# Other byte residues for the matmuls' normalised inputs and activations

## The reference

```python
# first block, per layer l (DEPTH = 2, D_MODEL = 1024, SEQ = 256)
h = rms_norm(x, norm_mix_g[l])
p = h @ w_in[l]                        # 1024 x 2832: convolution, attention, gated linear attention
y = concatenate([y_a, y_b, y_c])       # y_a, y_b, y_c: the three mixers on columns of p
x = x + y @ w_out[l]
h = rms_norm(x, norm_ffn_g[l])
u = causal_depthwise_conv(h @ ffn_w_up[l], ...)            # 1024 x 5632, three taps
x = x + (silu(u[..., :2816]) * u[..., 2816:]) @ ffn_w_down[l]
...
# second block, per layer l, for the image x and the context h_ctx
x = swiglu_half_step(x, norm_g[l, 0], mod_x, 0, w_ffn_up[l, 0], w_ffn_down[l, 0])
h_ctx = swiglu_half_step(h_ctx, norm_g[l, 0], mod_c, 0, w_ffn_up[l, 0], w_ffn_down[l, 0])
px, pc = hx @ w_in[l], hc @ w_in[l]    # hx, hc: modulated norms; the same weights for both
...                                    # neighbourhood and windowed attention over image and context
x = x + mod_x[..., 5, :] * (attention @ w_out[l])
x = swiglu_half_step(x, norm_g[l, 2], mod_x, 6, w_ffn_up[l, 1], w_ffn_down[l, 1])
# the same for h_ctx, except in the last layer
```

## Time and profile before

| | us |
|---|---|
| device time, median of 3 runs (2548.97 to 2557.46) | 2553.96 |
| span of the profiled execution, first to last instruction | 2549.3 |
| TensorE, matmuls busy | 2391.4 (94%) |
| TensorE, weight loads busy | 2322.8 (91%) |
| VectorE busy | 1661.0 (65%) |
| ScalarE busy | 997.7 (39%) |
| GpSimd busy | 188.2 (7%) |

### The profile page before, as it was taken

How to read it: one execution, slowest core, us unless ns; L and a number is a source line. 1 busy time by engine, 2 the same in 40 slices (tenths; PEclk the granted TensorE clock), 3 DMA queues, 4 the chain that set the end, 5 groups by cost and what they waited for, 6 DMA issues and landing times. The chain is left out here.

```text
span 2549.3 us, 47682 instructions
## 1 busy us (share of the span) xinstructions
PE 2391.4 (94%) x20452; PEld 2322.8 (91%) x20452; DVE 1661.0 (65%) x2777; ACT 997.7 (39%) x1468; POOL 188.2 (7%) x300
## 2 busy tenths in 40 slices
PE   7989998899799999999788999998999998988999
PEld 7889997899799999899558999998999998967999
DVE  6789888788877777744775677776333336376554
ACT  6455664465432222322473222223222223145543
POOL 0000000370000000011000900000000000100000
PEclk9899998999899999999898999999999999999999
DMA  6246652456445555412001455552222222211454
GB/s 256 95 157 226 221 190 92 144 197 237 141 143 191 188 182 187 169 59 79 14 1 67 164 190 189 186 198 91 92 96 96 100 100 96 70 52 67 162 194 157
DMA packets 104306, 352.78 MB, mean 138 GB/s; under 512 B 18976, under 2 KB 19232, under 8 KB 103840
## 3 DMA queue, kind: packets, MB, share of 16 engines
q1 hardware_dynamic: 95904, 348.94, 38.9%
q0 software_dynamic: 8192, 0.80, 0.3%
HBM read 348.63 MB, written 1.05 MB: 137 GB/s over the span
## 5 line engine op out<-in xcount | busy, mean ns | idle before, releaser
L1456 ACT ACTIVATE W_hi<-W_raw 128x1024 fp32r<-128x1024 f32 x510 | 538.7, 1060 | 1119.6 <-PE slot L930 1053.9
L1830 DVE TENSOR_TENSOR W_lo<-W_raw,W_hi 128x1024 fp32r<-128x1024 f32 x510 | 621.5, 1222 | 473.8 <-ACT W_hi L1456 465.1
L928 PE MATMUL slot<-H_hiA,W_lo 128*128 128x256 f32 x2768 | 790.9, 286 | 18.0 <-DVE H_loA L1960 4.6
L929 PE MATMUL slot<-H_loA,W_hi 128*128 128x256 f32 x2768 | 781.5, 282 | 0.0
L930 PE MATMUL slot<-H_hiA,W_hi 128*128 128x256 f32 x2768 | 780.9, 282 | 0.0
L928 PEld LDWEIGHTS slot<-H_hiA,W_lo 128*128 128x128 f32 x2768 | 533.3, 193 | 29.5 <-issue 21.1
L929 PEld LDWEIGHTS slot<-H_loA,W_hi 128*128 128x128 f32 x2768 | 535.8, 194 | 0.1
L930 PEld LDWEIGHTS slot<-H_hiA,W_hi 128*128 128x128 f32 x2768 | 532.7, 192 | 0.0
L1842 DVE SCALAR_TENSOR_TENSOR PROD<-A_raw,SC 128x1024 bf16<-128x1024 f32 x288 | 341.2, 1222 | 170.3 <-DMA A_raw<-adastream 169.8
L928 PE MATMUL slot<-H_hiB,W_lo 128*128 128x256 f32 x1376 | 385.9, 280 | 3.0 <-DVE VB L2347 1.3
L929 PE MATMUL slot<-H_loB,W_hi 128*128 128x256 f32 x1376 | 383.9, 279 | 0.0
(11 more groups left out here) (277 smaller groups left out, 3057.8 us busy)
## 6 DMA issues: line engine op xcount, KB each, us to landing
W_raw<-wstream SPq DMA_DIRECT2D x510, 512.0 KB, 3.3
A_raw<-adastream SPq DMA_DIRECT2D x144, 512.0 KB, 4.3
BT<-par POOLq DMA_DIRECT2D x256, 3.0 KB, 2.6
XA<-xT SPq DMA_DIRECT2D x2, 512.0 KB, 4.5
SC<-cond SPq DMA_DIRECT2D x1, 1024.0 KB, 14.4
XB<-ctxT SPq DMA_DIRECT2D x1, 1024.0 KB, 16.4
CON<-const SPq DMA_DIRECT2D x1, 960.5 KB, 9.6
PAR<-par SPq DMA_DIRECT2D x1, 680.0 KB, 10.8
```

Source lines behind the costliest of these rows:

```text
L928: pe.matmul(out, wl, xh, start=start, stop=False, skip_group_check=True)
L929: pe.matmul(out, wh, xl, start=False, stop=False, skip_group_check=True)
L1456: act.activation(W_hi[:, g % HIGH, :], W_raw[:, g % RAW, :], ACT.Copy).then_inc(S.w_hi, 1)
L1830: dve.tensor_tensor(W_lo[:, g % RAW, :], W_raw[:, g % RAW, :], W_hi[:, g % HIGH, :].bitcast(F32), ALU.subtract).then_inc(S.w_lo, 1)
```

## The change

A's `H` moves from 192 to 160, B's `H` to 224, A's arena to 32 and B's arena to 96 bytes modulo 256. To make room, what lies behind the arenas moves up by 256 bytes and so keeps its residue: the ring for the modulation's weights `A_raw`, its products `PROD`, the condition `SC`, the small tensors, and `X` of both streams. Nothing else differs.

```diff
-        A_raw = at("A_raw", 166 * K + 256, [P, ADA_RING, UNIT])
-        PROD = at("PROD", 174 * K + 256, [P, 2, UNIT], BF16)
-        SC = at("SC", 178 * K + 256, [P, 2, D])
-        small = [186 * K + 256]
+        A_raw = at("A_raw", 166 * K + 512, [P, ADA_RING, UNIT])
+        PROD = at("PROD", 174 * K + 512, [P, 2, UNIT], BF16)
+        SC = at("SC", 178 * K + 512, [P, 2, D])
+        small = [186 * K + 512]
...
-        AA, AB = 72 * K + 192, 124 * K + 192
-        for s, h_at, x_at, arena in ((A, 40 * K + 192, 150 * K + 256, AA), (B, 56 * K + 192, 158 * K + 256, AB)):
+        AA, AB = 72 * K + 288, 124 * K + 352
+        for s, h_at, x_at, arena in ((A, 40 * K + 160, 150 * K + 512, AA), (B, 56 * K + 224, 158 * K + 512, AB)):
```

## The result

The changed kernel takes 2602.10 us, median of 4 runs (2597.61 to 2607.36), beside 2551.47 us for the kernel before in the same runs (2536.46 to 2557.46, 4 runs). The ratio is 1.0205 with a 95% interval of 1.0157 to 1.0253: slower, by about 50 us. The forecast was 2554.0 us, so the time lies above the range of 2520 to 2588 as well.

The account below looks back on a forecast made before the run. The prediction took TensorE's matmul pace as the bound: long steps costing 27.9 us in joint stages plus 13.0 us solo, 40.9 against 36.2 before, add 4.7 to 2549.3, giving 2554.0 us; range 2520 to 2588.

Parts of the forecast that it names:

- the price of the new residues: TensorE's four moving operands: starting at 32 modulo 64 was taken to cost zero of its own.
- one long step each way: Bound on a new residue's price: -4.3 to +4.3 ns a matmul, the gap between steps of about 113.3 and 117.7 ns.
- The forecast is wrong if a third step appears: Sign of failure: any matmul-to-matmul step besides the short one (113.3 ns) and the long one (about 117.7 ns).
- The bound now: Whole kernel: the pace of TensorE's matmuls limits the time; waits were left as they are.
- What the long step cost before: Kernel before: matmuls at about 117.7 instead of 113.3 ns were put at 36.2 us in all.
- The switches: Joint stages: each change between streams A and B moves the residue 64 bytes and can re-choose the short or long step.
- the share of 0.55 long: Joint stages: 0.55 of 11,808 matmuls would run at the long step, costing 27.9 us.
- VectorE, ScalarE and small tensors at nothing: Other engines' work on moved tiles, and tensors moved by 256 bytes, taken at zero; 2% at most, 3 us.
- Rival 1: The new residues lock TensorE in the short step: 2526 us (joint stages alone) or 2513 us (everywhere); chance 0.28.
- Rival 2: Operands starting 32 bytes off a multiple of 64 need one more read step, locking the long step: 2590 us; chance 0.20.
- Rival 3: Residues don't matter and restarts alone set the rhythm: 2549 to 2554 us; chance 0.10.

Follow-up runs that it names:

- experiment 10: Kernel before with only the ring of W_raw and W_lo moved by 128 bytes (distance 64 to W_lo, 192 to W_hi): 2529.41 us, ratio 0.9889.
- Experiment 2: Kernel before with both H tiles and both arenas at one residue, 160, modulo 256: 2600.05 us, ratio 1.0153.
- experiments 1: Kernel before with all four tiles at multiples of 64 (H of A 128, H of B 192, arenas 0 and 64): 2595.08 us, ratio 1.0138.
- experiment 3: Kernel before with weight rings and tiles shifted together by 32 bytes (rings 32, tiles 224, distance still 192): 2547.91 us, ratio 0.9979.
- experiment 9: Kernel before with only the ring of W_raw and W_lo moved by 64 bytes (distance 128 to W_lo, 192 to W_hi): 2596.70 us, ratio 1.0143.

## Why the prediction was wrong

**The step that failed** is the price of the new residues: "That a residue of 32 modulo 64 has a price of its own no row shows ... I take zero, since two residues 64 bytes apart gave the same two steps to 0.2 ns." The two residues in the earlier trace rows belonged to distances 192 and 64. These are the only two of the ten distances in the table that allow 113.3 ns. From the two that share the pair of steps I concluded that all do. The bound was wrong with it: one long step each way, 4.3 ns over the short one. In the changed kernel the steps lie 3.4 to 6.7 ns over the short one, 5.1 ns in the mean: 17,378 x 5.1 = 89 us over an all-short kernel, where as many steps, all long, would be 17,378 x 4.3 = 75 us over it. The prediction named the sign of its own failure: "The forecast is wrong if a third step appears."

**The bound now.** Right: TensorE's pace, not the waits, set the end. The longest wait stayed within 0.2 us, and 55.4 us of change lie in the steps. Too simple was to add the steps to the span in full: 46.5 us of the changed kernel's 55.4 are in its span, and in experiment 10 steps shorter by 1.7 ns, 29 us in all, made the span shorter by 18.1. Where the rest went no run separates.

**What the long step cost before.** The forecast put 36.2 us on it; 17,365 steps at 115.34 instead of 113.33 ns are 34.9 us. Right as a sum of steps.

**The switches.** Right in structure: the step is chosen anew where the streams switch, as the visits to HIDB and HIDA show. Wrong in what they choose between, so the share of 0.55 long had nothing to apply to. Experiment 2 shows besides that the switches are not what costs.

**VectorE, ScalarE and small tensors at nothing.** Right: 1.3 us and less over the span, and 0.8% on the taps.

**The rivals.** Rival 1 fell: no tile locked the short step. Rival 2 came nearest in size (2590, span 2595.8), but its mechanism fell in experiments 1 and 3: multiples of 64 lose as well, and operands off them need not. Rival 3 fell: residues matter, as the relation of two addresses. The Trainium skill's page "SBUF — State Buffer" says under "Who interferes with whom" that TensorE has two independent read ports and never waits on anyone. The measurement decides otherwise for what TensorE does to itself: with the same instructions and a granted clock of 1.00, the distance of its two operands moved the step from 113.3 to 120.0 ns. That the ports are where this happens, no run here shows.

**What stays open.** That the two reads of TensorE, of moving data and of weights, get in each other's way is the reading that fits a distance. No run shows where: each distance has been seen from outside only, as a step. Why 64 and 192 differ in the step that a restart ends in, and why one load in three at another distance spoils the other two in experiment 9 and keeps all three short in experiment 10, is open as well.

## What to carry to other kernels

Where matmuls and weight loads follow each other without a gap, divide a window's length by its count of matmuls for each moving tile by itself; a few ns from tile to tile or from stage to stage, at one clock and without waits, point to where operands lie. Then treat the distance between moving and stationary operand, modulo 256 bytes, as a parameter to be tried, for each ring by itself: here it was worth some 3% between the changed kernel and the best layout with not one instruction changed. And a price for an address that no row has had is unknown on both sides; two addresses that behave alike say nothing about a third.

## What the runs showed of the hardware that was not expected

- Sixteen bytes of distance are enough: 192 allows 113.3 ns, 176 and 208 gave 116.6 to 119.5 ns.
- A third and fourth step exist, and at one distance several can occur (160: 117.3, 118.7, 120.0 ns), each held from restart to restart.
- Times of the kernel before ran from 2528 to 2577 us over all comparisons. The granted clock does not follow them (2527.90 and 2573.98 us both had 0.964), the share of long steps can: in experiment 3, at the same distances, the profiled execution had a mean step of 114.04 instead of 115.34 ns and a span 13.0 us shorter. That the whole spread comes from it is not shown. The layout of experiment 10, where the short step comes every time, ran within 2523.07 to 2532.99 us (4 runs).
- The load's duration follows the step only in part: 188 ns at both 113.3 and 116.8 ns, 191 ns at 120.0 ns.
